# Two-layer diffusion backbone on one core: the feed-forward nets' last value unit made bank by bank

## What is computed

```python
def conv_ffn(z, w_up, conv_w, conv_b, w_down):
    u = dwconv(z @ w_up, conv_w, conv_b, FFN_CONV // 2)
    g, v = jnp.split(u, 2, axis=-1)
    return (jax.nn.silu(g) * v) @ w_down

for l in range(DEPTH):
    ...
    zl = modulate(rmsnorm(xl, norm2_g[l]), mods[3], mods[4])
    xl = xl + mods[5] * conv_ffn(zl, ffn_w_up[l], ffn_conv_w[l], ffn_conv_b[l], ffn_w_down[l])
    ...
return rmsnorm(xl, final_g)
```

## Time and profile before

| | |
|---|---|
| median of 3 runs | 3203.03 us (3201.62 to 3203.48) |
| the profiled execution, its own time | 3201.8 us |
| its span in the trace | 3199.9 us |
| mean granted clock of PE | 0.981 |
| PE busy | 3039.0 us, 95% |
| DVE busy | 1585.4 us, 50% |
| ACT busy | 1065.1 us, 33% |
| POOL busy | 347.9 us, 11% |

### The profile page before, as it was taken

One profiled execution on the slowest core, in us unless ns is written; L12 is line 12 of the kernel. 1 busy time (PEld: TensorE's weight loads), 2 busy tenths in 40 slices (PEclk: granted clock), 3 DMA queues, 4 the chain that ended last, 5 costly groups with the idle time before them and its releaser, 6 DMA issues. The chain is left out here.

```text
span 3199.9 us, 39957 instructions
## 1 busy us (share of the span) xinstructions
PE 3039.0 (95%) x17039; PEld 2501.5 (78%) x17039; DVE 1585.4 (50%) x1953; ACT 1065.1 (33%) x1233; POOL 347.9 (11%) x363
## 2 busy tenths in 40 slices
PE   3699999999999999999989999999799999999997
PEld 2588787878888888888868888888687888887886
DVE  3667667264454444444564333333436554544545
ACT  2478675131121221111244444444323212222122
POOL 0122221200000000000043222222010000000002
PEclk8899999999999999999999999999998999999998
DMA  7244433322212211212111111111131111111111
GB/s 257 63 128 122 129 104 115 107 73 73 66 54 66 66 60 53 66 60 66 46 58 27 38 37 36 36 39 39 41 124 40 46 46 53 47 46 47 46 46 53
DMA packets 216875, 217.88 MB, mean 68 GB/s; under 512 B 34302, under 2 KB 191581, under 8 KB 210555
## 3 DMA queue, kind: packets, MB, share of 16 engines
q1 hardware_dynamic: 206155, 160.07, 16.5%
q0 software_dynamic: 10192, 55.21, 5.3%
q10 hardware_dynamic: 352, 0.06, 0.0%
HBM read 190.27 MB, written 25.03 MB: 67 GB/s over the span
## 5 line engine op out<-in xcount | busy, mean ns | idle before, releaser
L749 PE MATMUL ps<-zH,wH 128*128 128x512 f32 (+1 forms) x2136 | 575.7, 369 | 12.5 <-DVE zL L627 11.1
L749 PE MATMUL ps<-zH,wL 128*128 128x512 f32 (+1 forms) x2136 | 572.4, 368 | 0.0
L749 PE MATMUL ps<-zL,wH 128*128 128x512 f32 (+1 forms) x2136 | 571.8, 367 | 0.0
L749 PEld LDWEIGHTS ps<-zH,wH 128*128 128x128 f32 x2136 | 369.3, 188 | 102.1 <-issue 23.7
L749 PEld LDWEIGHTS ps<-zH,wL 128*128 128x128 f32 x2136 | 369.4, 188 | 69.7
L749 PEld LDWEIGHTS ps<-zL,wH 128*128 128x128 f32 x2136 | 369.3, 188 | 69.5
L2166 DVE SCALAR_TENSOR_TENSOR res<-ps,mod,res 128x1024 f32<-128x1024 f32 x240 | 236.7, 1014 | 189.6 <-PE ps L749 178.3
L759 DVE SCALAR_TENSOR_TENSOR V<-ps,vec,V 128x1023 f32<-128x1023 f32 (+1 forms) x132 | 134.1, 1016 | 391.9 <-ACT V L2039 388.8
L2015 ACT ACTIVATE wH<-wraw 128x1024 fp32r<-128x1024 f32 x130 | 134.6, 1050 | 391.8 <-PE ps L749 391.8
L749 PE MATMUL ps<-hH,wH 128*128 128x512 f32 (+1 forms) x700 | 193.1, 373 | 0.0
L749 PE MATMUL ps<-hL,wH 128*128 128x512 f32 (+1 forms) x700 | 191.0, 370 | 0.0
(11 more groups left out here) (315 smaller groups left out, 4659.6 us busy)
## 6 DMA issues: line engine op xcount, KB each, us to landing
wraw<-in_ffn_w_up_dram SPq DMA_DIRECT2D x88, 512.0 KB, 3.9
modw<-in_mod_w_dram POOLq DMA_DIRECT2D x40, 1024.0 KB, 5.2
wraw<-in_ffn_w_down_dram SPq DMA_DIRECT2D x44, 512.0 KB, 3.6
wraw<-in_na_w_in_dram SPq DMA_DIRECT2D x24, 512.0 KB, 4.8
modring<-in_mod_w_dram SPq DMA_DIRECT2D x8, 1024.0 KB, 8.8
wraw<-in_rg_w_in_dram SPq DMA_DIRECT2D x16, 512.0 KB, 5.0
bias<-scratch_bias SPq DMA_DIRECT2D x32, 224.0 KB, 4.1
scratch_xT<-res SPq DMA_DIRECT2D x8, 640.0 KB, 7.3
```

Source lines behind the costliest of these rows:

```text
L749: last = nc.tensor.matmul(ps[:, slot * SLOT + c:slot * SLOT + c + n], w(k), r(k)[:, c:c + n], start=(k == 0 and i == 0), stop=(k == K - 1 ...
```

## The change

1. The last value unit (group 10, v1) of both nets is made bank by bank: PE does all 24 matmuls of bank 0, then those of bank 1 (and of bank 2), and reports each bank. ACT and DVE follow by bank, with a function `last_unit` each. A bank's last column needs its right neighbour from the next bank, so bank 0 is treated up to column 510, and column 511 (`edge`) gets its right tap, gate, `hH` and `hL` as operations of one column, once bank 1 is there.
2. The items of piece c wait for `h_ready` of `KF + c`, so item (0, 0) waits for bank 0 with its edge column alone.
3. In the tail `sums` of piece 0 stands ahead of item (1, 5) in the first net and (1, 4) in the second, instead of (1, 3); `spread` of piece 0 three items later, that is ahead of (2, 0) and (1, 7), instead of (1, 6).
`LATE` is 5 in the first net and 4 in the second. In the diff the first piece of `last_unit` is ACT's, the second DVE's.
4. On DVE more additions stand ahead of `inverse(0)`; on ACT the order of squares and `z_high` changes accordingly. ACT's first weight split of the attention stands behind the first eight squares instead of ahead of them; its other half (`wL`) goes from POOL to DVE, behind item (1, 3)'s addition.

```diff
-        pe.wait_ge(h_ready, KF)
         for c in range(tail.n):
+            pe.wait_ge(h_ready, KF + c)
             for mt in range(KD):
-                if (c, mt) == (1, 3):
+                if (c, mt) == (1, LATE):
                     tail.sums(pe, 0, tail_sq(0, KD - 1), KD, KD)
-                if (c, mt) == (1, 6):
+                if KD * c + mt == KD + LATE + 3:
                     tail.spread(pe, 0)
...
+                    if (i, kind, j) == LAST:
+                        for c, (at, n) in enumerate(banks):
+                            for q in range(KD):
+                                ins = piece_steps(nc, m, 3 * s, c, at, n, q, wH, wL)
+                            ins.then_inc(unit_done, 1)
...
+            for c, (at, n) in enumerate(banks):
+                act.wait_ge(unit_done, done + c)
+                if c > 0 and at in edge:
+                    high(full, at - 1, at)
+                    full += 1
+                nc.scalar.activation(m.V[:, at:at + n], src[:, at:at + n], ACT.Identity, scale=fcol(m, l, 1, col), bias=fcol(m, l, 3, col)).then_inc(mid, 1)
+                high(full, at, at + n - (at + n in edge))
+                full += 1
...
+            for c, (at, n) in enumerate(banks):
+                if at in edge:
+
+                    dve.wait_ge(unit_done, done + c)
+                    tap(1, at - 1, at)
+                    gate(at - 1, at)
+                    low(at - 1, at).then_inc(h_ready, 1)
+                end = at + n - (at + n in edge)
+                dve.wait_ge(mid, 2 * KF + c)
+                tap(-1, at + (at in (0, SEQ)), at + n)
+                tap(1, at, at + n - 1)
+                if c == len(banks) - 1:
+                    dve.nop().then_inc(psum_free[slot], 1)
+                gate(at, end)
+                ins = low(at, end)
+                if end == at + n:
+                    ins.then_inc(h_ready, 1)
...
     def early_gpsimd(gp):
-        w_low(gp, 0)
+        pass
+
+    def early_vector(dve):
+        dve.wait_ge(w_high, 1)
+        nc.vector.tensor_tensor(m.wL[:, place(0), :], m.wraw[:, place(0), :], m.wH[:, place(0), :].bitcast(F32), ALU.subtract).then_inc(w_ready, 1)
```

More of the change, by code:

```diff
@@ L1821, in ffn @@
     bank_free = sem(tag + "bank_free")
+    LAST = (NG - 1, "v", 1)
+    edge = [c + n for c, n in banks if c + n < SEQ]
+    LATE = 5 if tail.n == 3 else 4
     def program(eng, group):
@@ L1876, in gpsimd @@
         tail.clear(gp)
-        nxt.early_gpsimd(gp)
         for c in range(tail.n):
+            if c == 1:
+                nxt.early_gpsimd(gp)
             for mt in range(KD - 1):
@@ L2053, in group, with last_unit, high @@
                     k += 2
+        def last_unit(src, done, col):
+            def high(n, at, end):
+                act.wait_ge(h_full, KF + n)
+                nc.scalar.activation(m.hH[:, 1, at:end], m.V[:, at:end], ACT.Copy).then_inc(h_high, 1)
+            full = 0
+            for c, (at, n) in enumerate(banks):
[6 more added lines that the diff above has]
+                full += 1
         def after(first, i, u0, k):
@@ L2071, in scalar @@
         program(act, group)
-        nxt.early_scalar(act)
         act.wait_ge(h_ready, KF)
@@ L2076, in scalar @@
             square(0, mt)
+        nxt.early_scalar(act)
         for mt in range(3):
@@ L2079, in scalar @@
         tail.root(act, 0)
-        for mt in range(3, 6):
+        for mt in range(3, KD):
             square(1, mt)
@@ L2083, in scalar @@
             tail.z_high(act, 0)
-            square(1, 6)
+            square(2, 0)
             tail.z_high(act, 1)
-            square(1, 7)
+            square(2, 1)
             tail.z_high(act, 2)
-            square(2, 0)
-            square(2, 1)
+            square(2, 2)
             tail.z_high(act, 3)
-            for mt in range(2, KD):
+            for mt in range(3, KD):
                 square(2, mt)
             tail.root(act, 1)
-        else:
-            square(1, 6)
-            square(1, 7)
     def early_vector(dve):
@@ L2139, in group @@
                     col = 2 * i + ((0 if kind == "g" else KF) + j)
+                    if (i, kind, j) == LAST:
+                        last_unit(order, src, u0 + u + 1, col, s)
+                        continue
                     if part_ is BODY and (kind, j) == ("g", 0):
@@ L2177, in group, with last_unit, gate, low @@
                     k += 2
+        def last_unit(order, src, done, col, slot):
+            full = 0
+            def gate(at, end):
+                nonlocal full
+                nc.vector.tensor_tensor(m.V[:, at:end], m.V[:, at:end], m.G[:, at:end], ALU.mult).then_inc(h_full, 1)
+                full += 1
+            def low(at, end):
+                dve.wait_ge(h_high, KF - 1 + full)
+                return nc.vector.tensor_tensor(m.hL[:, 1, at:end], m.V[:, at:end], m.hH[:, 1, at:end].bitcast(F32), ALU.subtract)
+            def tap(shift, at, end):
+                order(nc.vector.scalar_tensor_tensor(out=m.V[:, at:end], in0=src[:, at + shift:end + shift], scalar=fcol(m, l, 1 + shift, col),
+                                                     in1=m.V[:, at:end], op0=ALU.mult, op1=ALU.add))
+            dve.wait_ge(silu_done, KF)
+            for c, (at, n) in enumerate(banks):
[14 more added lines that the diff above has]
+                    ins.then_inc(h_ready, 1)
         def taps_by_bank(order, dst, col):
@@ L2219, in vector @@
             add(0, mt)
-        for mt in range(3):
-            add(1, mt)
-        tail.inverse(dve, 0)
-        for mt in range(3, 6):
+        for mt in range(4):
             add(1, mt)
         if tail.n == 3:
-            tail.z(dve, 0)
+            nxt.early_vector(dve)
+            add(1, 4)
+            add(1, 5)
+            tail.inverse(dve, 0)
             add(1, 6)
-            tail.z(dve, 1)
             add(1, 7)
-            tail.z(dve, 2)
-            add(2, 0)
-            add(2, 1)
-            tail.z(dve, 3)
-            add(2, 2)
-            add(2, 3)
+            for mt in range(4):
+                tail.z(dve, mt)
+                add(2, mt)
             tail.z(dve, 4)
@@ L2240, in vector @@
         else:
+            add(1, 4)
+            tail.inverse(dve, 0)
+            add(1, 5)
+            add(1, 6)
             nxt.early_vector(dve, 0)
-            add(1, 6)
+            add(1, 7)
             nxt.early_vector(dve, 1)
-            add(1, 7)
     part.mod_used = mod_used
@@ L2651, in vector @@
         out(NP - 1, NR - 1)
-    part.early_scalar, part.early_gpsimd = early_scalar, early_gpsimd
+    part.early_scalar, part.early_gpsimd, part.early_vector = early_scalar, early_gpsimd, early_vector
     part.sync, part.scalar, part.gpsimd, part.tensor, part.vector = sync, scalar, gpsimd, tensor, vector
```

8 lines of the change are left out of this document (7 added, 1 removed).

## The result

| | before | change |
|---|---|---|
| median | 3203.09 us (3201.62 to 3203.48, 4 runs) | 3182.36 us (3180.99 to 3183.58, 4 runs) |
| profiled execution, its own time | 3201.8 us | 3180.99 us |
| its span | 3199.9 us | 3179.0 us |
| mean granted clock of PE | 0.981 | 0.984 |

The ratio is 0.9936 (95% interval 0.9919 to 0.9953): 20.7 us less, where 18 were forecast, inside the range (3182 to 3190) but near its low end.

The account below looks back on a forecast made before the run. With the tensor engine busy 95% of the span, only its idle or low-clock time at the nets' ends could give much. 8.0 us (second net) + 10 (first) = 18: 3201.8 becomes 3183.8 profiled, 3185.0 median; range 3182 to 3190.

Parts of the forecast that it names:

- Entry, second net: Second net, start of the tail: only the edge column stays on PE's path, 0.9 us; first sums gain 8.7 us.
- Exit, second net: Second net, from the first sums on: two chains run to the end, the later one sets a gain of 8.0 us.
- chain (b): Second net's exit on DVE: seven `scaled` behind the last addition instead of six, ending 8.0 us earlier; the later chain.
- chain (a): Second net's exit: root, then squares and POOL's additions, then the second sums; a gain of 9.0 us.
- First net: First net's tail: PE doesn't stop ahead of its items and gains 11.2 us; 10 us taken at the exit.
- The forecast cover at the sums: First net: POOL's seven additions end at 1624.3, ahead of the first sums at 1625.6; cover 1.3 us.
- the exit: First net, DVE decides: the last addition ends 9.7 us earlier, between 8.3 and 10.7; 10 us taken.
- the first `zH` behind five squares: First net's exit: `zH` waits behind piece 1's squares, the last waiting for POOL; costs 1.0 us (0 to 2.4).
- The second spread's wait: First net: PE's wait grows to 4.5 us but stays ahead of DVE's `z`, so it costs nothing.
- The rival of 4 us: DVE and POOL block each other at two `zL`, split and additions: 4 us lost, gain 14, 3189 us; chance 0.19.
- its bound for this rule: DVE and POOL exclude each other for whole instructions: five `zL` could each lose up to 1.4 us, gain 11.
- The sum: Both nets' tails together: 8.0 + 10 = 18 us less.

Follow-up runs that it names:

- the unit alone: Last unit by bank and items waiting by piece, but the tail in its old order, against the kernel before: 3188.49 us, ratio 0.9956.

## Why the prediction was right, and where its steps were off

**Entry, second net.** The edge took the 0.9 us forecast. The first item started 11.88 us behind the last G instead of 18.63: 6.8 us earlier, as forecast (3139.7 for 3146.58). The first sums, one item later, came 28.32 behind the last G, before 35.38; with the item's 1.36 us that is a gain of 8.4 instead of 8.7. POOL's seven additions ended 0.9 us ahead of them (3142.68, sums at 3143.55); 0.65 was forecast.

**Exit, second net.** The forecast was 8.0 by chain (b). The last `scaled` ended 42.04 us behind the last G (3157.27 less 3115.23), before 49.82 (3177.77 less 3127.95): 7.8. But the tail as cut gained 6.96, since the root came 0.80 us late: the second sums ran at 1.2 GHz, 3.5 us (3154.20 to 3157.75) instead of 1.9. In the repeat of the change they ran at 2.4 GHz and the reciprocal followed the last `scaled` at once (41.97). The step that was missing is that sums at a low clock let chain (a) overtake chain (b). Seven profiles have this second tail, all with a wait of 2.30 to 2.32 us ahead of the second sums. The clock fell from 0.1 us ahead of them to 2.6 us behind their start, and the tail followed: 42.85 and 42.83 us where it fell first, 42.68, 42.59 and 42.32 at 0.2, 0.3 and 0.6 us, 41.96 and 41.97 at 1.1 and 2.6. The change was at both ends of this in its two executions, so the low clock's place there differs from execution to execution.

**First net.** PE had no idle time ahead of the first item. The forecast cover at the sums was 1.3 us; it was 1.24, since POOL's seventh addition ended at 1624.50 (9.93 behind 1614.57) and the sums began at 1625.74. For the exit I took 10 us from between 8.3 and 10.7; it was 10.6 (11.2 in the repeat). The step that was mis-sized is the first `zH` behind five squares: priced at 1.0 us, while from the first `z` to the last addition's end it took 10.3 us, with 10.1 + 1.0 forecast. That `zH` did start late (1634.04, when the first `z` had ended at 1633.47), but DVE had the next addition and the next `z` to do meanwhile and stood idle only 0.22 us ahead of the first `zL` (1634.78). The second spread's wait, forecast as 4.5 us, was 1.77. PE got there later than reckoned, as 256-wide items ran at 1.2 GHz (the 3.4 us from 1638.60, so 1.7 us), and the last addition ended about a microsecond earlier than forecast. With `LATE` 4, where the clock did not fall there, PE waited 4.83. It cost nothing in the change because DVE, not PE, was on the path.

**Blocking.** The rival of 4 us did not come. The four `zL` ahead of the last addition took 0.75, 0.74, 1.03 and 0.74 us, the diagonal 1.04 instead of 0.69, the split on DVE 1.79. DVE's timeline of the change:

```profile
1625.24 1.79 DVE L2416 TENSOR_TENSOR wL<-wraw,wH 128x1024 fp32r<-128x1024 f32 x1
...
1638.22 1.03 DVE L725 SCALAR_TENSOR_TENSOR zL<-ztmp_t,mod,zH 128x512 fp32r<-128x512 f32 x1
...
1643.88 1.04 DVE L686 TENSOR_TENSOR diag_p<-ident,root 128x512 f32<-128x512 f32 x1
...
1645.50 2.67 DVE L725 SCALAR_TENSOR_TENSOR zL<-ztmp_t,mod,zH 128x512 fp32r<-128x512 f32 x1
```

The 2.67 us lie under POOL's split of the next weight (1645.27, 2.36 us); before, the same split made a `zL` of 2.00 us, so the change pays 0.67 us more there. Where a `zL` was not held up, POOL's timeline shows why:

```profile
1633.56 1.30 POOL L657 TENSOR_TENSOR acc<-acc,sq_t 128x512 f32<-128x512 f32 x1
...
1635.00 1.68 POOL L657 TENSOR_TENSOR acc<-acc,sq_t 128x512 f32<-128x512 f32 x1
```

The first `zL` (1634.78 to 1635.53) was already running when this addition started, and the addition took 1.68 us instead of 1.30. The block is there, but whoever starts second pays. From the split on DVE to the second diagonal that was POOL five times (additions of 2.08, 1.50 and 1.68 us instead of 1.30, and of 1.00 and 1.30 instead of 0.73) and DVE three times (the split, one `zL`, the diagonal). That one waits for the other's whole instruction agrees with the Trainium skill (SBUF — State Buffer, SBUF: two separate sides), which gives the ports to the one that starts first; my price of a whole addition for each meeting put every meeting on DVE. The prediction also counted five `zL` up to the last addition; there are four, since each `zL` follows the next `z`, so its bound for this rule should have been 12.4 us of gain, not 11.

**The sum.** The two tails give 10.6 + 7.0 = 17.6 us in the recorded pair, 11.2 + 8.1 = 19.3 in the repeats; 18 were forecast. The rest of the recorded pair's 20.8 is outside the tails: 2.77 between the nets and 2.01 at the end, less 0.60 at the start, 0.07 in the second net's body and 0.9 behind the last copy. The 2.01 are chance: the stretch from the second reciprocal to the last copy took 15.4 to 17.5 us over twelve profiles with the same end, 16.4 on average both in the six whose second tail kept its old length and in the other six, and in the repeats it was longer in the change (17.35 to 15.97). So 20.7 against 18 is partly luck of the pair; the repeats give 19.4. Between the nets lies a part that the change does not touch; what differs there is the clock. Stretches of 35 us at the same place of the attention, before and change:

```profile
2405.00:2440.00 35.00, 28.50 (x106) 20.96 (x105) 21.86 (x33) 13.66 (x20) 1.17 (x1) 0.76 0.10 30
```
```profile
2394.50:2429.50 35.00, 28.35 (x115) 20.67 (x114) 23.93 (x36) 14.30 (x21) 1.17 (x1) 0.85 0.10 30
```

and in the kernel with the weight split on POOL, whose first tail is as short as the change's:

```profile
2395.00:2430.00 35.00, 28.74 (x106) 20.99 (x105) 21.86 (x33) 13.23 (x19) 1.17 (x1) 0.76 0.11 30
```

The low clock holds for 17.1 us there before and for 10.2 in the change. Over all 14 profiled executions the stretch between the nets took 763.6 to 764.5 us in the five whose first tail kept its old length (mean 764.1) and 761.7 to 764.4 in the nine with a shorter one (mean 762.8). The length goes with the low clock in this one place, not with the tail: 764.1 to 764.5 us in the six profiles with 17.1 us of it, 763.5 and 763.6 in the two with 13.7, 761.7 to 762.4 in the six with 10.2. All six with 10.2 have a short first tail, but two with a short tail (the unit alone, the split on POOL) had 17.1 all the same. So some 1.3 us may come with the earlier arrival, or by chance; that stays open. The prediction had no term for it.

## What to carry to other kernels

Where a chain of engines drains a long tensor-engine unit and nothing else is left to run, cut the unit by bank and let the consumer wait by bank too: in the second net the cut alone gave nothing, the two together all of the gain. Then move the small reductions behind by the same amount, on every engine's queue at once: here one item on PE alone cost 3 us, 2 of them because DVE's queue still expected the old place; with DVE's moved, its waits for ACT, whose queue was left, took 2.0. Price an idle time of the tensor engine with the low clock behind it, and look where that low stretch falls: under sums that others wait for it costs the whole chain. Where it falls differs between executions of one kernel, so a gain or loss of up to 2 us in one profile is not yet the edit's.

## What was not expected of the hardware

- The clock fell to 1.2 GHz for 6.8 us at the end of a wait of only 2.15 us at the sums (the unit alone) and of 2.32 us (second sums, second net; in the repeat, after 2.30 us, these sums still ran at 2.4 GHz and the clock fell behind them), and for 3.4 us behind one of 0.56 us followed by 16 matmuls of one column, while it stayed at 2.4 GHz behind the 1.04 us ahead of the first item.
- Avoiding one low stretch did not avoid the next: with PE kept busy in the gap, the items gained 1.65 us, but the low stretch at the second sums, 3.4 us from 2.0 us behind their start before, was 6.8 us from 0.7 us behind it.
- When a `zL` and an addition of POOL meet, POOL pays at least as often as DVE: 1.68 us instead of 1.30 for its addition.
- Operations of one column are cheap on both engines: 0.16 to 0.22 us on DVE, 0.20 on ACT, against 0.69 (a gate) and 0.63 for 511 columns.
